# Norm of the meta tokens on Pool, their turn behind tile 1, and eight turns of the identity ahead of the first weights

## The reference

```python
def rmsnorm(x, g):
    xf = x.astype(jnp.float32)
    y = xf * lax.rsqrt(jnp.mean(xf * xf, axis=-1, keepdims=True) + EPS)
    return (y * g.astype(jnp.float32)).astype(x.dtype)

h = jnp.concatenate([zeros(PAD), meta_tokens, x], axis=1)
u = rmsnorm(h, norm_g[l])
proj = jnp.einsum('bld,de->ble', u, w_in[l])      # ten projections of width 1024
# branch A: gated linear recurrence over chunks; branch B: differential attention
# m = sigmoid(ga) * yA + sigmoid(gb) * yB; h = h + m @ w_out; out = rmsnorm(h, final_g)
```

## Time and profile before

| | us |
|---|---|
| median of three runs (lowest, highest) | 703.93 (703.45, 704.18) |
| the profiled execution | 702.9 |
| its span, first to last instruction | 701.1 |
| busy in the span: TensorE, its weight loads | 682.5, 644.2 |
| busy: VectorE, ScalarE, Pool | 562.4, 462.5, 172.9 |
| mean granted TensorE clock, as a share of full speed | 0.999 |

### The profile page before, as it was taken

How to read it: one execution, slowest core, us unless ns; L and a number is a source line. 1 busy time by engine, 2 the same in 40 slices (tenths; PEclk the granted TensorE clock), 3 DMA queues, 4 the chain that set the end, 5 groups by cost and what they waited for, 6 DMA issues and landing times.

```text
span 701.1 us, 15657 instructions
## 1 busy us (share of the span) xinstructions
PE 682.5 (97%) x5097; PEld 644.2 (92%) x5097; DVE 562.4 (80%) x1276; ACT 462.5 (66%) x1028; POOL 172.9 (25%) x196
## 2 busy tenths in 40 slices
PE   3999999999999999999999999999999999999996
PEld 2998999999999999999999999999999988888884
DVE  5889869978978987997997897898667745766796
ACT  6463876886796697688588669668767653333454
POOL 2012333233333243223323333333411000000001
PEclk9999999999999999999999999999999999999999
DMA  8347668877967967886886797788786544235713
GB/s 335 129 103 180 141 151 187 172 191 174 203 142 175 223 154 165 173 187 179 163 196 154 183 203 163 166 188 203 156 214 176 163 152 148 91 120 121 240 31 121
DMA packets 52234, 117.69 MB, mean 168 GB/s; under 512 B 5826, under 2 KB 6228, under 8 KB 52196
## 3 DMA queue, kind: packets, MB, share of 16 engines
q0 software_dynamic: 23328, 44.05, 37.5%
q1 hardware_dynamic: 28548, 72.75, 30.4%
q10 hardware_dynamic: 320, 0.39, 0.2%
HBM read 71.03 MB, written 2.10 MB: 104 GB/s over the span
## 4 chain that ended last, share of the span: by engine, by line
PE 95%; DVE 1%; DMA 1%; issue 1%; ACT 1%; POOL 0%; SPq 0%; POOLq 0%; DVEq 0%; ACTq 0%
PE ps L765 26%; PE ps L767 25%; PE ps L766 25%; PE ps L946 3%; PE ps L1021 3%; PE ps L1049 3%; PE ps L928 1%; PE ps L1038 1%; PE ps L982 1%; PE ps L1050 1%; PE ps L981 1%; PE ps L991 1%; PE ps L962 1%; DMA x_in<-in_x 1%; PE ps L971 1%
## 5 line engine op out<-in xcount | busy, mean ns | idle before, releaser
L408 ACT ACTIVATE w_hi<-w_raw 128x512 fp32r<-128x512 f32 x216 | 132.6, 623 | 61.4 <-PE ps L767 29.0
L765 PE MATMUL ps<-t_hi,w_hi 128*128 128x256 f32 x576 | 168.9, 293 | 0.0
L765 PE MATMUL ps<-uT_hi,w_hi 128*128 128x272 f32 (+3 forms) x536 | 163.7, 305 | 2.6 <-DVE uT_lo L1779 2.4
L767 PE MATMUL ps<-t_hi,w_lo 128*128 128x256 f32 x576 | 162.6, 282 | 0.0
L766 PE MATMUL ps<-t_lo,w_hi 128*128 128x256 f32 x576 | 162.6, 282 | 0.0
L767 PE MATMUL ps<-uT_hi,w_lo 128*128 128x272 f32 (+3 forms) x536 | 155.5, 290 | 0.0
L766 PE MATMUL ps<-uT_lo,w_hi 128*128 128x272 f32 (+3 forms) x536 | 155.5, 290 | 0.0
L680 POOL DMA_DIRECT2D w_lo<-w_raw x84 | 79.2, 943 | 181.2 <-ACT w_lo L410 168.9
L765 PEld LDWEIGHTS ps<-t_hi,w_hi 128*128 128x128 f32 x576 | 109.7, 190 | 3.0 <-issue 2.0
L766 PEld LDWEIGHTS ps<-t_lo,w_hi 128*128 128x128 f32 x576 | 109.8, 191 | 0.0
L767 PEld LDWEIGHTS ps<-t_hi,w_lo 128*128 128x128 f32 x576 | 109.8, 191 | 0.0
(11 more groups left out here) (301 smaller groups left out, 1498.3 us busy)
## 6 DMA issues: line engine op xcount, KB each, us to landing
w_raw<-in_w_in SPq DMA_DIRECT2D x44, 512.0 KB, 4.8
w_lo<-w_raw POOLq DMA_DIRECT2D x84, 256.0 KB, 4.3
w_raw<-in_w_in SPq DMA_DIRECT2D x72, 256.0 KB, 4.4
w_sum<-in_w_in SPq DMA_DIRECT2D x36, 256.0 KB, 3.2
w_raw<-w_raw POOLq DMA_DIRECT2D x36, 256.0 KB, 3.5
w_sum<-w_raw POOLq DMA_DIRECT2D x36, 256.0 KB, 4.8
w_raw<-in_w_branch_a SPq DMA_DIRECT2D x8, 512.0 KB, 3.2
w_raw<-in_w_branch_b SPq DMA_DIRECT2D x8, 512.0 KB, 3.3
```

Source lines behind the costliest of these rows:

```text
L408: act.activation(part_at(w_hi, j), part_src(pr, j), ACT.Copy).then_inc(pair_hi[j], 1)
L765: pe.matmul(dst, w[0], rhs[0], start=start, stop=False, skip_group_check=True)
L767: return pe.matmul(dst, w[1], rhs[0], start=False, stop=stop, skip_group_check=True)
```

## The change

Four lists are edited.

- Pool: behind the power of tile 1 (`n == 2`) it makes the meta tokens' norm in two products over 16x1024: meta times gain into a new buffer `x_sq2`, and that times the number of each token, back into `x_in`. Two new semaphores, `meta_gained` between the two and `meta_normed` behind them.
- VectorE: `norm_x(1)` is gone. `TURNED = (0, 1, CH, 2, 3)` takes the place of `X_ORDER` in both `turned_x`, so the meta tokens' low half now comes behind tile 1's; `mean_x(3)` moves ahead of tile 1's.
- ScalarE: `square_x(3)` moves ahead of `turned_x(1)`, which is now tile 1, and the meta tokens' copy stands behind that, ahead of `square_x(4)`.
- TensorE: the meta tokens are turned behind tile 1 and the small rows, waiting for `meta_normed`, and eight turns of the identity into bank 2, which nothing reads, stand between them and `half_section(0, 0)`.

```diff
+FILLERS = 8
+TURNED = (0, 1, CH, 2, 3)
...
+    x_sq2, o2 = at("x_sq2", [P, D], F32, o2)
...
                 pool.tensor_tensor(rstd[0:m, i:i + 1], ms[0:m, i:i + 1], half_neg[0:m, 0:1], ALU.pow) \
                     .then_inc(x_rstd, 1)
+                if n == 2:
+                    pool.wait_ge(norm_in, 16)
+                    pool.wait_ge(x_rstd, 2)
+                    meta = x_in[0:META, CH, :]
+                    pool.tensor_tensor(x_sq2[0:META, :], meta, g_in[0:META, :], ALU.mult).then_inc(meta_gained, 1)
+                    pool.wait_ge(meta_gained, 1)
+                    pool.tensor_scalar(meta, x_sq2[0:META, :], rstd[0:META, CH:CH + 1], None, ALU.mult) \
+                        .then_inc(meta_normed, 1)
...
             def turn_x(n):
-                i = X_ORDER[n]
+                i = TURNED[n]
                 if n == 0:
                     pe.wait_ge(x_half, 1)
+                elif i == CH:
+                    pe.wait_ge(meta_normed, 1)
                 else:
-                    pe.wait_ge(x_normed, n + 1)
+                    pe.wait_ge(x_normed, i + 1)
...
             turn_x(0)
             turn_x(1)
-            turn_x(2)
             pe.wait_ge(rows_ready, 48)
             pe.transpose(bank(1)[:, 0:2 * HEADS + 2], rows_in[:, :], ident[0:2 * HEADS + 2, 0:2 * HEADS + 2]) \
                 .then_inc(pe_pre, 1)
+            turn_x(2)
+            for k in range(FILLERS):
+                pe.transpose(bank(2)[:, k % 4 * P:(k % 4 + 1) * P], ident[:, :], ident[:, :])
             half_section(0, 0)
...
             unit_hi(act, 0, 1, 3, None)
+            square_x(3)
             turned_x(1)
-            square_x(3)
             turned_x(2)
             square_x(4)
...
             mean_x(2)
-            norm_x(1)
             norm_x(2)
             turned_x(0)
             unit_lo(dve, 1, 0, 3, lo_ready)
+            mean_x(3)
             turned_x(1)
-            mean_x(3)
             turned_x(2)
             mean_x(4)
```

More of the change, by code:

```diff
@@ L305, in build @@
     x_half = sem("x_half")
+    meta_gained, meta_normed = sem("meta_gained"), sem("meta_normed")
     u_ready_hi, u_ready_lo = sem("u_ready_hi"), sem("u_ready_lo")
@@ L770, in turn_x @@
             def turn_x(n):
-                i = X_ORDER[n]
+                i = TURNED[n]
                 if n == 0:
                     pe.wait_ge(x_half, 1)
+                elif i == CH:
+                    pe.wait_ge(meta_normed, 1)
                 else:
-                    pe.wait_ge(x_normed, n + 1)
+                    pe.wait_ge(x_normed, i + 1)
                 if i in (2, 3):
-                    pe.wait_ge(u_ready_lo, X_ORDER.index(i - 2) + 1)
+                    pe.wait_ge(u_ready_lo, TURNED.index(i - 2) + 1)
                 for k in range(KT):
```

## The result

| | before | after |
|---|---|---|
| median of 16 runs each, same chip (lowest, highest), us | 703.45 (702.81, 704.29) | 704.94 (704.03, 706.16) |
| profiled execution, us | 702.9 | 706.16 |
| its span, us | 701.1 | 704.3 |
| TensorE's waits for tiles 0 and 1, us | 7.5, 0.7 | 8.2, 3.3 |
| TensorE back after the second departure, us | 26.34 | 27.75 |

The ratio after over before is 1.0017 [1.001, 1.0023]: slower by 1.2 us [0.7, 1.6]. The forecast was 705.2 and +1.3. The profiled execution is the slowest of its sixteen, so its span must not be read as the change's worth.

A forecast was written before the change was run, and what follows sets the result against it. TensorE was taken as the bound, so the change moves its return at 26.34. Pool's second product ending at 16.0 instead of allowing 14.65 gives +1.3; median 703.93 + 1.3 = 705.2 us, range 703.1 to 706.4.

The forecast's parts named there:

- T: End of Pool's second product, releasing TensorE's turns of the meta tokens; forecast at 16.0 us.
- Pool's power back to 0.55: Pool's power for tile 1, without VectorE's meta product beside it, takes 0.55 us instead of 1.52.
- VectorE's norm of tile 1 first: VectorE's norm starts at 10.08, ahead of Pool's first product asking at 10.17, so that product reads only from 11.36.
- the second rival: Pool's first product asks first and holds VectorE, so tile 1 is normed at 12.3 to 13.6: +1.2, 705.1; chance 0.13.
- First product 2.3: Pool's first product, meta times gain, costs 2.3 us, the middle of 1.4 and 3.2.
- Second product 1.4: Pool's second product, with each token's number, costs 1.4 us, being most like the memset.
- Weight low held from 13.5 to 14.7: VectorE's first weight low, due at 12.5, waits for Pool's first product until 13.5 and ends at 14.7.
- Mean of tile 3 at T + 2.64 = 18.6: VectorE's mean of tile 3 follows T by 2.64 us, through turns, ScalarE's copy and square; 16.72 before.
- Return at T − 14.65 = +1.3, 27.7: TensorE's return after its second departure, 26.34 before, moves by T − 14.65, +1.3 us, through VectorE's list.
- Fillers neutral, covered by VectorE's late list: Eight identity turns ahead of TensorE's first weights cost nothing; the 24 matmuls end at 22.2, needed by 23.0.
- No mutual hold: Rival: Pool's products run from 10.04 at once, T = 13.75; change -0.9, time 703.0; chance 0.28.
- The fillers don't wake the clock: Rival: TensorE's pace rises only at 22.3, 14 matmuls slow, end at 23.5; +1.8, 705.7; chance 0.09.

The follow-up runs named there:

- e3: Changed kernel with Pool's first product made to wait until VectorE has normed tile 1; ratio to before 1.0036, +2.5 us.
- e5: Changed kernel with Pool's two products removed and the meta norm back on VectorE, behind tile 1's; ratio to before 0.9988, 0.8 us faster.
- e8: Changed kernel with Pool's two products over 512 of the 1024 columns; ratio to before 0.9989, 2.0 us below the changed kernel.
- e1: Changed kernel without the eight turns of the identity (the fillers); ratio to before 1.0018, +1.3 us.
- e10: Changed kernel with VectorE's first weight low moved ahead into Pool's second product; single execution, weight low 2.07 us instead of 1.21.
- e11: Changed kernel once more, unedited, for a second profile; ratio to before 1.0016, +1.1 us.
- e4: Kernel before plus three unread Pool operations over 16x1024 at the start; memset 0.95 us, product with a number per token 2.85, product of two tensors 1.88.
- e2: Kernel before plus only the eight turns of the identity ahead of the first weights; ratio to before 0.9981, 1.3 us faster.
- e6: e2 with one VectorE weight low moved between the norms of tiles 2 and 3; ratio to before 0.9984.
- e7: Kernel before with 4, 2 and 9 turns of the identity in TensorE's three gaps; ratio to before 0.9978.
- e9: e5 with the weight-low move of e6 and six turns of the identity in each of two places; ratio to before 0.999.
- e12: e9 without the move of the weight low; ratio to before 0.998.

## Why the prediction was right

The result is where the forecast put it (+1.3 against +1.2 [0.7, 1.6]), and its cause is the stated one: Pool's two products end late and TensorE pays for it (e3, e5, e8). The sum that gave the number is right in part by luck. On the way to T the order of the two engines, the price of the second product and the hold on the weight low were wrong and cancelled out. Behind T, the link through VectorE's list was not the one that ended last; TensorE's own row, which the forecast took to be covered, was the later one by up to 0.2 us (item 8).

1. *Pool's power back to 0.55.* Right, 0.55 at 9.43.
2. *VectorE's norm of tile 1 first.* Wrong. Pool's first product starts right as its power ends, 9.95, while VectorE needs the semaphore, 10.02; Pool comes first. This was the second rival (0.13). In all profiles of the changed order it went so (after, e1, e8, e10, e11). The forecast had counted 0.13 from Pool's start to its request, which would put Pool's at 10.08, behind VectorE's start, and nothing like it for VectorE; no row shows how long VectorE takes from its start to its request.
3. *First product 2.3.* Right, 2.35. The Trainium skill's "GPSIMD Engine Reference" (3.1, Elementwise) has 4497 ns for an add of two tensors of 2048 elements (the forecast calls it a product); half of it, an estimate of 2.25, agrees with the 2.35 of the trace. But the forecast's own reckoning, the middle of 1.4 and 3.2, was not what made it right: from 512 to 1024 columns (e8 and after) this product grows from 1.26 to 2.35, so 2.1 ns an element and little besides.
4. *Second product 1.4.* Wrong, 2.85 (e4). This is the term most out of size: "most like the memset" was the reason, and the product is not. The error is 1.45 us. By the same two runs (1.45 of work in e8, 2.73 in after) it is 2.5 ns an element, where the memset has 0.87.
5. *Weight low held from 13.5 to 14.7.* Wrong in the changed kernel (14.50, 1.21), because VectorE reaches it late in the second product. Where Pool is second (e3), it was held as the forecast said.
6. *T = 16.0.* Measured 16.11 by another sum: 12.10 (Pool's first product lets go) + 1.28 (the norm) + 2.73. The forecast's own was 13.5 + 1.2 + 1.27. Its road with the true prices is 17.97 (e3). By its terms, the second product was priced 1.45 too low and the 1.2 of the weight low never came in between; the two errors cancel, and the order of the norm and the first product hardly changes their sum. So T was right by luck; the road of the rival with the second product at 1.27 would have given 14.65.
7. *Mean of tile 3 at T + 2.64 = 18.6.* Right: 18.57, and T + 2.46 both there and in e3. In e8, where T is 13.63, it no longer follows T.
8. *Return at T − 14.65 = +1.3, 27.7, through VectorE's list, "as long as TensorE's own row keeps up".* Measured 27.75, but TensorE's row did not quite keep up. It should have ended its 24 matmuls at 22.2 against a limit of 23.0 and ended them at 23.10, since the pace rose at 21.3, not 19.3. In e5 VectorE goes on to its last `uT_lo` 0.06 us after the start of the instruction before it; by that VectorE's list alone would have put the return of after near 27.55 (an estimate). In all six profiles with Pool's products VectorE stands still ahead of that `uT_lo` and waits for TensorE's turns: about 0.1 us in after, 0.20 in e8, 0.59 in e1, 0.75 in e11, 0.79 in e10, 1.01 in e3. So T reaches the return by TensorE's own row: meta turns behind T, the fillers, the 24 matmuls at whatever pace they get. In after, before, e1, e2, e3, e4, e8, e10 and e11 the return comes 4.65 to 4.67 us behind the start of the turns that follow the 24 matmuls (23.10 and 27.75; the earlier trace rows: 21.68 and 26.34). VectorE's list is the later one only in e5, e6, e7 and e9, all without Pool's products; in e12 the distance is 4.79, with the first of those turns still slow. That the two roads end within 0.2 us of each other in after is the second piece of luck: in e11, the same kernel, the return is +1.97.
9. *Fillers neutral, covered by VectorE's late list.* Neutral is right in the timed runs (e1), the reason is not: TensorE's row is the later one with them and without them. Without them, 20 of the 24 matmuls run at the slow pace (e1), with them 10 or 16 (after, e11), and this fills much of the time that the fillers took.
10. *Rivals.* No mutual hold (703.0) is refuted by 3.36 and 3.71. "The fillers don't wake the clock" is not clean: the pace rose late in after (21.3, forecast of that rival 22.3) and at 22.6 in e11, but inside the turns in e6 and e9. The Trainium skill's "TensorE: Matmul & The Clock Gate" (Part 4: PE-mode transpose) has it that transposes don't count as TensorE work here; in e6, e9 and e12 the pace rose before any weight matmul had run, so the measurement decides against the sentence as it stands, if these turns are of the kind it means: the trace calls them MATMUL and doesn't tell. That they raise it each time isn't shown either: e2 and e6 have the same list on TensorE up to 17 us and rise at 21.7 and about 16.

What stays open: what sets the moment of the rise (12 to 25 us over all profiles; 21.3 and 22.6 for one kernel, about 16 and 21.7 for the same list up to 17 us), and whether a gap of 1.4 us makes it fall (e12) or not (e9), and why e2 is faster by 1.3 us in the timed runs and not in its profile up to 27 us. From the return to ScalarE's first square of the final norm, near the end of the kernel, before takes 652.7 us, after 654.9, e11 653.7, e7 653.5, e1 652.9: some of what is won or lost early may be evened out or added in the heads. No rule is seen in it, and no run was made for it. So the return in one profile tells the road of the change, and its worth is told by the timed runs alone.

## What to carry to other kernels

An instruction given to Pool to relieve VectorE can hold VectorE up: here Pool's first product cost VectorE 2.1 us of standing still for 1.26 of work taken away. Price each kind of Pool instruction by one probe before moving it; the one with a number per token was the dearest though it reads least. And where the end of one instruction frees the next one on its own engine and, by a semaphore, one on another engine, ask which has its next instruction already in its own queue: here Pool had, and it came first in all five profiles. Last, when a sum has two roads that end close together, work out both with their measured terms; the one taken to be covered can be the one that decides.

## What was new of the hardware

- Pool on 16x1024 f32, alone (e4): memset 0.95 us, product with a number per partition 2.85, product of a tensor with itself 1.88. Product of two tensors, with VectorE held up by it: 2.35 (after, e3). The "GPSIMD Engine Reference" of the Trainium skill (4.1) calls a one-input operation roughly line-rate; the 2.85 stands against it.
- The hold between the two engines goes both ways. The Trainium skill's "SBUF — State Buffer" (Who interferes with whom) says of VectorE's two-port mode that whoever issues first has the shared ports for the whole instruction and the other is fully blocked; of a VectorE instruction with two SBUF inputs it says that it contends with a Pool instruction that reads SBUF, and calls the shared ports an exclusive lock in general. The forecast read the whole length into both cases. For the product of two tensors this nearly fits (weight low held to 14.03 of a product that ends at 14.16, e3; the norm to 12.10 of 12.30, after). For the product with a number it doesn't: 0.86 of 2.85 (e10).
- Two VectorE instructions with two SBUF inputs each, back to back, keep a Pool power out through both: 2.66 us for it in e9 against 1.52 behind one.
- The pace rose in turns alone (e6, e9, e12). After 1.41 us without TensorE work it was low again in e12, with 24 matmuls at the slow pace behind it; after 1.42 us at the same place in e9 it was not.
